# Expert weights loaded as whole rows, and the three products of an expert put in another order

## What is computed

```python
def ec_moe(h, w_router, w_gate, w_up, w_down):      # 16 experts, all weights 1024 x 1024, float32
    cap = EC_CAPACITY_FACTOR * t // N_EXPERTS       # 64 rows an expert (and 32 context rows in the first layer)
    aff = softmax(h @ w_router)
    gates, idx = lax.top_k(swapaxes(aff, 1, 2), cap)
    xs = h[idx]                                     # the chosen rows of each expert
    a = einsum('becd,edf->becf', xs, w_gate)
    u = einsum('becd,edf->becf', xs, w_up)
    y = einsum('becf,efd->becd', silu(a) * u, w_down)
    y = y * gates[..., None]
    return zeros.at[idx].add(y)
```

## Time and profile before

| | |
|---|---|
| three runs | 2847.03, 2845.25, 2837.01 us; median 2845.25 |
| the profiled execution | 2837.34 us; its span is 2836.0 us, the 1.3 us beside it lie around the span |
| granted TensorE clock, mean | 0.953 |
| layer 0: `turn_x` of expert 0 to that of expert 15 | 1052.8 to 1626.5 us |
| layer 1: `turn_x` of expert 1 to that of expert 15 | 2269.6 to 2777.8 us |

### The profile page before, as it was taken

How to read it: one execution, slowest core, us unless ns; L and a number is a source line. 1 busy time by engine, 2 the same in 40 slices (tenths; PEclk the granted TensorE clock), 3 DMA queues, 4 the chain that set the end, 5 groups by cost and what they waited for, 6 DMA issues and landing times.

```text
span 2836.0 us, 28948 instructions
## 1 busy us (share of the span) xinstructions
PE 2519.1 (89%) x11063; PEld 1642.9 (58%) x11063; DVE 1785.5 (63%) x2790; ACT 1403.6 (49%) x2004; POOL 296.7 (10%) x268
## 2 busy tenths in 40 slices
PE   5998898999899859999999977799998499999998
PEld 2444444456685326666666644566763377777776
DVE  2147425258653157888888854666631688888987
ACT  2024322125442127777777752444421377777775
POOL 0000000001101101112122100000000111111221
PEclk9999999999999879999999998999998799999999
DMA  6123410110000388999999991000016599999997
GB/s 248 61 88 110 158 63 22 52 60 1 1 1 2 139 298 296 349 354 355 341 348 352 350 339 56 1 1 1 1 61 246 190 356 366 359 360 346 369 363 246
DMA packets 233243, 546.46 MB, mean 193 GB/s; under 512 B 9289, under 2 KB 12169, under 8 KB 232978
## 3 DMA queue, kind: packets, MB, share of 16 engines
q1 hardware_dynamic: 221122, 518.94, 50.6%
q0 software_dynamic: 6144, 20.98, 3.2%
q10 hardware_dynamic: 5840, 4.70, 0.5%
HBM read 523.62 MB, written 20.97 MB: 192 GB/s over the span
## 4 chain that ended last, share of the span: by engine, by line
PE 57%; DVE 16%; DMA 14%; ACT 8%; issue 4%; ACTq 0%; POOL 0%; SPq 0%; DVEq 0%; POOLq 0%
PE PS L1833 16%; DMA AR<-in_w_exp_down_dram 7%; PE PS L1457 7%; DVE RW L1804 6%; PE PS L620 6%; PE PS L643 6%; PE PS L787 5%; ACT RW L1796 3%; PE PS L631 3%; PE PS L1164 2%; DMA AR<-in_w_ada_dram 2%; ACT AR L1893 2%; PE PS L998 2%; PE PS L396 2%; DMA AR<-in_w_exp_up_dram 1%
## 5 line engine op out<-in xcount | busy, mean ns | idle before, releaser
L1804 DVE TENSOR_TENSOR RW<-AR,RW 128x2048 fp32r<-128x2048 f32 x384 | 871.1, 2286 | 129.7 <-ACT RW L1796 128.3
L1796 ACT CAST RW<-AR 128x2048 fp32r<-128x2048 f32 x384 | 731.0, 1912 | 330.9 <-PE PS L1833 184.3
L1833 PE MATMUL PS<-RW,RX 128*96 128x512 f32 (+1 forms) x3072 | 751.4, 399 | 62.6 <-issue 35.7
L1833 PEld LDWEIGHTS PS<-RW,RX 128*96 128x96 f32 (+1 forms) x3072 | 533.2, 176 | 249.4 <-issue 62.1
L1833 PE MATMUL PS<-RW,RA 128*96 128x512 f32 (+1 forms) x1536 | 369.0, 396 | 7.4 <-DVE RA L1949 7.4
L1833 PEld LDWEIGHTS PS<-RW,RA 128*96 128x96 f32 (+1 forms) x1536 | 265.3, 175 | 96.2 <-DVE RA L1949 14.6
L620 PE MATMUL PS<-AR 128*128 128x256 f32 (+5 forms) x640 | 236.5, 487 | 7.1 <-ACT AR L663 3.8
L663 ACT ACTIVATE AR<-PS,AR 128x768 f32<-128x768 f32 (+1 forms) x160 | 130.4, 815 | 218.7 <-DVE AR L713 134.5
L643 PE MATMUL PS<-AR 128*128 128x128 f32 x1600 | 210.4, 279 | 5.8 <-DVE AR L745 4.3
L643 PEld LDWEIGHTS PS<-AR 128*128 128x128 f32 x1600 | 194.3, 194 | 16.9 <-issue 15.5
L1457 PE MATMUL PS<-AR 128*128 128x512 f32 (+1 forms) x480 | 193.6, 560 | 3.3 <-DMA AR<-in_w_in_even_dram 3.3
(11 more groups left out here) (303 smaller groups left out, 2433.9 us busy)
## 6 DMA issues: line engine op xcount, KB each, us to landing
AR<-in_w_exp_gate_dram SPq DMA_DIRECT2D x64, 2048.0 KB, 9.4
AR<-in_w_exp_up_dram SPq DMA_DIRECT2D x64, 2048.0 KB, 10.2
AR<-in_w_exp_down_dram SPq DMA_DIRECT2D x64, 2048.0 KB, 9.9
AR<-in_w_ada_dram SPq DMA_DIRECT2D x30, 2048.0 KB, 8.2
AR<-in_w_in_dram SPq DMA_DIRECT2D x6, 2048.0 KB, 7.9
AR<-in_w_in_even_dram SPq DMA_DIRECT2D x4, 2048.0 KB, 8.3
AR<-in_w_out_dram SPq DMA_DIRECT2D x2, 2048.0 KB, 8.5
AR<-in_w_out_even_dram SPq DMA_DIRECT2D x2, 2048.0 KB, 7.7
```

Of the source, the lines that this page charges most:

```text
L1796: s.copy(pair(i)[0], raw_half(key, hf)).then_inc(*S.up("hi", l, i))
L1804: v.tensor_tensor(lo, raw_half(key, hf), hi.bitcast(F32), ALU.subtract).then_inc(*V.up("split", key, hf))
L1833: m = pe.matmul(bank(ob)[0:Mc, :], st_, mv[:, k, 512 * q_:512 * q_ + 512], start=(first and k == 0 and n_ == 0), stop=(last and k == nk - ...
```

## The change

Every half of an expert matrix is now 512 whole rows, taken as `"(p c) n -> p (c n)"`: partition p gets rows 4p to 4p+3, one run of 16 KB. The rows of a chunk c are then 4p+c instead of 128c+p, so each transpose that makes the other operand takes every fourth column (`perm`), in `turn_x`, in `turn_a`, and in the transposes ahead of the router. Bias and norm columns of these layers are made in the same order.

Since a load now holds rows for all 1024 columns, gate and up each fill two banks over two loads, as down did before. The order becomes: up of expert e (two loads), first load of gate of expert e+1, `turn_a` of e (8 transposes at once), second load of gate e+1, first load of down e, `turn_x` of e+2, second load of down e. The tanh is one instruction of 1024 columns; the multiplications stand two by two after the second load of gate and of up. The last expert has no gate of a next one: its `turn_a` stands directly behind its up.

```diff
+def perm(k):
+    return slice(512 * (k // 4) + k % 4, 512 * (k // 4) + 512, 4)
...
-        def down_load(l, e, h):
-            src = T["w_exp_down_2"][l, e, h * 512:h * 512 + 512, :].rearrange("(c p) n -> p c n", p=128)
-            cyc(("down", l, e, h), src, (4, 1024), three)
+        def expert_load(nm, l, e):
+            for h in range(2):
+                src = T[f"w_exp_{nm}_2"][l, e, h * 512:h * 512 + 512, :].rearrange("(p c) n -> p (c n)", c=4)
+                cyc((nm, l, e, h), src, (4, 1024), three)
 
         def expert_loads(l):
+            expert_load("gate", l, 0)
             for e in range(16):
-                for h in range(2):
-                    for nm in ("gate", "up"):
-                        colchunk((nm, l, e, h), T[f"w_exp_{nm}_2"][l, e], h * 512, h * 512 + 512, three)
-                    pe_, ph = (e, 0) if h else (e - 1, 1)
-                    if pe_ >= 0:
-                        down_load(l, pe_, ph)
-            down_load(l, 15, 1)
+                expert_load("up", l, e)
+                if e < 15:
+                    expert_load("gate", l, e + 1)
+                expert_load("down", l, e)
...
-        def moe_order(l):
-
-            o = []
+        def moe_order():
+
+
+            o = [("turn_x", 0, 0), ("gate", 0, 0), ("gate", 0, 1), ("turn_x", 1, 0)]
             for e in range(16):
-                o += [("gate", e, 0)] + ([("turn_a", e - 1, 1)] if e else []) + [("up", e, 0)]
-                if e:
-                    o += [("down", e - 1, 1)]
-                o += [("gate", e, 1), ("turn_a", e, 0), ("up", e, 1)]
-                if e + 1 < 16:
-                    o += [("turn_x", e + 1, 0)]
+                o += [("up", e, 0), ("up", e, 1)]
+                if e < 15:
+                    o += [("gate", e + 1, 0), ("turn_a", e, 0), ("gate", e + 1, 1)]
+                else:
+                    o += [("turn_a", e, 0)]
                 o += [("down", e, 0)]
-            return [("turn_x", 0, 0)] + o + [("turn_a", 15, 1), ("down", 15, 1)]
+                if e + 2 < 16:
+                    o += [("turn_x", e + 2, 0)]
+                o += [("down", e, 1)]
+            return o
...
-                                             xs[e % 2][:, 128 * (4 * hf + k):128 * (4 * hf + k) + 128], ident[0:R, 0:R])
+                            m = pe.transpose(bank(b)[:, R * k:R * k + R], xs[e % 2][:, perm(4 * hf + k)],
+                                             ident[0:R, 0:R])
...
                 elif kind == "turn_a":
-                    nb_ += 1
-                    b = K.fill(6 + nb_ % 2, "ta", l, e, h)
-                    P.wait_ge("read", "u", l, e, h)
-                    for k in range(4):
-                        m = pe.transpose(bank(b)[:, R * k:R * k + R], ac[h][:, 128 * k:128 * k + 128], ident[0:R, 0:R])
-                    m.then_inc(*K.full("ta", l, e, h))
+                    P.wait_ge("read", "up", l, e, 0)
+                    P.wait_ge("read", "up", l, e, 1)
+                    for hf in range(2):
+                        nb_ += 1
+                        b = K.fill(6 + nb_ % 2, "ta", l, e, hf)
+                        for k in range(4):
+                            m = pe.transpose(bank(b)[:, R * k:R * k + R], ac[e % 2][:, perm(4 * hf + k)],
+                                             ident[0:R, 0:R])
+                        m.then_inc(*K.full("ta", l, e, hf))
...
             for e in range(16):
-                if e:
-                    scatter(e - 1)
-                if 1 <= e + 1 < 15:
+                if e < 14:
                     gather(e + 2)
-            scatter(15)
+                scatter(e)
```

More of the change, by code:

```diff
@@ L360, in program @@
         BIAS_ROW = [a for a in ADA if a[1] in (2, 5)]
-        BIAS_COL = [a for a in ADA if a[1] not in (2, 5)]
+        BIAS_COL = [a for a in ADA if a[1] in (0, 1)]
+        BIAS_PERM = [a for a in ADA if a[1] in (3, 4)]
         def ada_groups(l, j):
@@ L1628, in piece_list @@
         def piece_list(l):
-            p = []
-            for e in range(16):
-                for h in range(2):
-                    for key in (("gate", l, e, h), ("up", l, e, h), ("down", l, e, 0) if h else ("down", l, e - 1, 1)):
-                        if key[2] >= 0:
-                            p += [(key, 0), (key, 1)]
-            return p + [(("down", l, 15, 1), 0), (("down", l, 15, 1), 1)]
+            return [(key, hf) for key, src in LOADS if key[0] in ("gate", "up", "down") and key[1] == l
+                    for hf in range(2)]
         PIECES = {l: piece_list(l) for l in range(2)}
@@ new lines, in pe_experts @@
+                    P.wait_ge("read", "up", l, e, 0)
+                    P.wait_ge("read", "up", l, e, 1)
+                    for hf in range(2):
+                        nb_ += 1
[4 more added lines that the diff above has]
+                        m.then_inc(*K.full("ta", l, e, hf))
+                else:
+                    b0 = {"gate": 0, "up": 2, "down": 4}[kind]
+                    if h == 0:
+                        for q_ in range(2):
+                            K.fill(b0 + q_, kind, l, e, q_)
+                    if kind == "down":
+                        P.wait_ge("read", "ta", l, e, 0)
+                        P.wait_ge("read", "ta", l, e, 1)
+                    else:
+                        P.wait_ge("xl", l, e)
+                    use((kind, l, e, h), [b0, b0 + 1], aF if kind == "down" else xF[e % 2])
@@ new lines, in dve_experts @@
+                if kind == "turn_a":
+                    hi, lo = hi_lo(aF, 8, R)
+                    for hf in range(2):
+                        V.wait_ge("ah", l, e, hf)
+                        v.tensor_tensor(lo[:, 4 * hf:4 * hf + 4, :], bank(V.bank_of(("ta", l, e, hf)))[:, 0:4 * R]
+                                        .rearrange("p (k c) -> p k c", c=R),
+                                        hi[:, 4 * hf:4 * hf + 4, :].bitcast(F32), ALU.subtract)\
+                            .then_inc(*V.read("ta", l, e, hf))
@@ L2482, in sync @@
                     sp_moe(0)
-                if key == ("up", 1, 0, 0):
+                if key == ("gate", 1, 0, 1):
                     sp_moe(1)
```

171 lines of the change are left out of this document (86 added, 85 removed).

## The result

| | before | after |
|---|---|---|
| median of 4 runs | 2841.39 us (2837.01 to 2847.03) | 2902.24 us (2888.80 to 2903.90) |
| ratio after / before, 95% interval | | 1.0203 [1.0165, 1.0241] |
| span of the profiled execution, mean granted clock | 2836.0 us, 0.953 | 2901.7 us, 0.943 |

The change makes the kernel some 2% slower. By landmarks of PE's queue (the first and the last matmul of each expert layer) the 65.7 us of the spans divide so: ahead of layer 0 +15.0, layer 0 (1066.1 to 1677.5 before, 1081.1 to 1726.9 after) +34.4, between the layers -0.2, layer 1 (2245.2 to 2828.8, then 2294.4 to 2894.5) +16.6, the end 0.

A forecast was written before the change was run, and what follows sets the result against it. It took DMA as a co-bound without reserve, beside PE's waits behind ACT's scaling burst. Terms -1.5 - 4 + 11 + 2 = +7.5 us, added to the mean 2843, gave 2850 us; range 2815 to 2885.

The forecast's parts named there:

- part 3: Expert weight loads: 16 KB runs save 0.25 us a load; periods 38.15 and 36.0 us, giving -1.5 and -4 us.
- Part 1: Behind turn_x in layer 0: PE's wait for xF becomes 2.7 us for p4, up's second weight piece; net 0.
- Part 2: Rest of an expert's period: ends at 37.6 us in layer 0, 0.1 below today's; 35.6 in layer 1.
- the walk: Step-by-step timing of ACT, PE and DVE over one expert's weight pieces: 37.6 us in layer 0, 35.6 in layer 1.
- the four distances under 10 us: Times from a load slot being freed to being wanted: 8.75, 8.35, 9.9, 9.3 us, against landings of 9.4 to 9.9.
- Part 4: End of each layer: no work covers the last expert's final turn; +5.4 us each, +11 for two.
- Part 5: Beginning of each layer: expert 1's turn comes later, about +1 us each; other sums under 1; +2 in all.
- Rival 1: Expert layers: ACT's scaling burst is absorbed, layers run at PE's 35.3 and 35.2 us; -46 us, 2797; chance 0.19.
- Rival 2: Transposes: loading every fourth float32 as stationary operand takes twice as long; +50 us, 2900; chance 0.12.
- Rival 3: Scatter and gather delay down's load; PE waits for turn_a's subtraction: every expert +57 us, half +28 (2872); chance 0.20.

The follow-up runs named there:

- e5: Changed kernel with the second half of turn_x's scalings, their cast and DVE's subtraction moved behind down's second load: 2878.79 us, ratio 1.0144.
- e9: Changed kernel with turn_x's scalings in three parts and expert 14's second down load multiplied ahead of the last turn_a: 2840.31 us, ratio 0.9999.
- e17: Changed kernel with extra matmuls in layer 0, ten ahead of up's second piece, five ahead of the turned activations' wait: 2908.37 us, ratio 1.0224.
- e19: Changed kernel with eight extra matmuls in layer 0, only in PE's wait ahead of up's second piece: 2898.58 us, ratio 1.0213.
- e18: Changed kernel, nothing altered, measured and profiled again: 2896.12 us, ratio 1.0171.
- e15: Changed kernel with each scatter held until PE has turned the next expert's activations, and gathers one expert earlier: 2894.93 us, ratio 1.0175.
- e11: Changed kernel with each expert scattering only 8 of its 96 or 64 rows: 2867.88 us, ratio 1.0075.
- e4: Changed kernel with plain transposes instead of every fourth column, 16 KB runs kept: 2887.24 us, ratio 1.0155.
- e12: Changed kernel with expert 14's second down load multiplied between the last up and the last turn in each layer: 2892.93 us, ratio 1.0181.
- e16: e9 with the scatter and gathers moved as in e15: 2833.35 us, ratio 0.9966.
- e2: Kernel before, own order and loads, with only the transposes of turn_x and turn_a taking every fourth column: 2848.84 us, ratio 1.0028.
- e14: e9 with plain transposes under the 16 KB layout: 2834.22 us, ratio 0.9972.
- e3: Changed kernel with 4 KB runs and plain transposes, so the new order alone: 2907.61 us, ratio 1.0244.
- e10: Kernel before, own order and loads, with turn_x in two halves, the first ahead of gate's second load: 2834.13 us, ratio 0.9973.

## Why the prediction was wrong

**Where the time went.** The last column of the table says it. 16 KB runs did make the transfers of an expert shorter, from 38.3 to 36.4 us, about as part 3 had it (1.5 for six loads). But the queues now stand idle 0.09 x 39.96 = 3.6 us of each period, where before the share was 1.00. The burst makes this hole: it holds back the piece whose second half frees the slot of gate's second load, so this load goes out 9.5 us after the one ahead of it. This much the rows show, and that the hole closes when the burst is spread (e5, e9) and stays when only PE's wait is filled (e17, e19), which gains nothing.

For the same reason a short period doesn't last. In the one of 38.17 us the queues moved 327 x 38.17 = 12.5 MB, in the next, of 42.86 us, 14.6; an expert needs 335 x 39.96 = 13.4. Each of the five periods under 39 us is followed by one of 40.6 to 42.9, and in e18 the five that have a next one by 40.7 to 43.0. So what the hole leaves undone comes as late loads in the next expert. Which load is late there is inferred: the loads of down follow close behind gate's second, beside scatter and gather, the next expert's up lands behind them, and so its burst starts late. Late down is no needed link (e15); fewer bytes help while the hole stays (e11).

**Part 1, right.** Predicted 2.7 us of wait for p4, ended by a weight piece; measured 2.33 to 2.42 in the undisturbed experts, and up to 4.1 where loads are late.

**Part 2, right for what it walked.** 37.6 us plus a stride of 0.4 gives 38.0; the undisturbed period is 38.17, and 37.8 in e4 without strides. In layer 1 the walk said 35.6; the shortest period is 35.8 in after and 35.3 in e4.

**Part 3, the step that failed:** "I set the period to 38.15 in layer 0 and 36.0 in layer 1". The means are 39.96 and 37.0. The excess is 1.8 x 15 + 1.0 x 14 = 41 us, four fifths of the miss of 52. The size taken for 16 KB runs was right, and the four distances under 10 us were seen. What was missing is that the walk started each expert with all loads in time, and took only the lateness of one load within one period. It did not ask what the queue does while the burst holds the slots (3.6 us of idle queue, priced at nothing), nor carry a late load into the next expert. Only 5 of the 13 periods of layer 0 stay below 39 us; the walk describes PE in these, and even in the one of 38.17 ACT waits 4.6 us for down. It also had no term for the clock. In the three periods of 39.55 us ACT waits for no load at all, and the 1.4 us over 38.17 are matmuls at the lower clock; it may be this delay that gives the loads their time. e17 and e19 show that without these falls the mean is the same. In layer 1 the time under half the DMA share is 1.5 us an expert, where before it was 0.04: a smaller hole of the same kind. The rest of the 1.0 us an expert there was not taken apart.

**Part 4, right.** +5.4 each: the wait grew from 1.73 to 7.45, +5.7 in layer 0, and from 1.56 to 6.7, +5.1 in layer 1. Most of it stands ahead of the turn (5.93 us; the walk had 5.65 there), and not behind it, where the prediction's list of signs looked for 7 to 8. That a cover is easy was not claimed, and e12 shows that it is not.

**Part 5, not settled.** It put +1 into the beginning of each layer and under 1 elsewhere. Ahead of layer 0 there are +4.0 in e18, and layer 0 is another 7 us (9 in e18) longer outside the 13 periods and the end. That holds the beginning and the two or three other experts, and was not taken apart.

**Rival 1** did not occur, and e16 shows what it would have taken: with the burst spread and the scatter moved, layer 0 does run at 36.3, near the 35.3 that the rival named. The change alone does neither.

**Rival 2, right in kind, mis-sized.** The weight load rose from 139 to 218 ns, 1.6 times and not twice. The cost is 0.3 to 0.9 us an expert by the shortest periods (e2 against before, after against e4, e9 against e14), 8 us of the time in e2 and 6 to 8 between e14 and e9, not 50. The Trainium skill, "SBUF — State Buffer", section Specifications (TRN2), has lines of 16 bytes that want two hits; the trace agrees in direction. The section gives no size; the factor of two was the prediction's own bound.

**Rival 3, right in its cause, not in its path.** Late loads of down are there (22 us of waits in after, 51 in e3), and scatter is what lies beside them (e11, e15). But its sign, PE waiting for `turn_a`'s subtraction ahead of down, is nowhere in the two stretches of 13 experts of after. It shows in e3 (16.8 us over the 13 experts of layer 0), and in e5 (20.4 us) once the burst is halved. Its full price, +57 at every expert, lies near the measured loss, but by another way, so that is luck. It had 0.20 and 2872 for half of the experts; this also leaves out the +7.5 of the prediction's own sum.

The Trainium skill, "DMA: Bandwidth & Descriptors", section Specifications, would have let the length of the runs buy nothing above 358 GB/s. Layer 0 of e16 moved 368 GB/s over 471 us, so here too the measurement decides; and in the new order 16 KB runs were worth 0.9% against 4 KB (e4 against e3).

**Left open.** No run closes the hole and leaves PE's wait as it is: e5 and e9 shrink both, e17 and e19 fill the wait alone. Layer 1 of the changed kernel is 17 to 19 us longer. Its 13 periods hold 8 (10 in e18), its bare end some 5 (a wait of 5.6 ahead of the last turn), the first experts the rest; which of their waits it is was not tried. What a fall of the clock would cost the whole program if the queue had room was not separated either.

**A version that beats both.** e16 (whole rows, new order, burst in three parts, scatter later) has a ratio of 0.9966 [0.9951, 0.9982] to before, and e10, before's own loads with the burst halved, 0.9973 [0.9957, 0.9988]. Both gains are 0.3%, and both compute what the kernel before computes.

## What to carry to other kernels

Where a kernel is bound by two things at once, walk the loads' queue like an engine: a small burst on ACT that delays the release of one buffer is a hole in the queue, and the queue gives it back as late loads, in the next iteration too. A good iteration proves nothing if it moved fewer bytes than an iteration needs. A faster transfer is worth only what the order lets it use: multiply the DMA share by the period before and after, and see whether work or idle time changed. Before covering a wait with other work, list what that work puts into the queues of the engines that end the wait.
